# A float32 block on one core: the activation buffers moved to another byte phase relative to the weights

## What is computed

```python
# first block
h = rmsnorm(x, g);   proj = h @ w_in                    # 1024 x 6144
x = x + (gates * (conv, pool and short-conv branches)) @ w_o
x = x + cross_attention(rmsnorm(x), rmsnorm(mem))       # w_xq, w_xkv, w_xo
x = x + moe(rmsnorm(x))      # 16 experts, top 2 of one group: silu(t @ gate) * (t @ up) @ down
x = rmsnorm(x, norm_f_g)
# second block
x = x + rmsnorm((axial attention and gated scan over h @ w_in_2) @ w_out_2)
x = x + rmsnorm(cross_attention_2(...))
x = x + rmsnorm(conv_ffn(...))   # 1024 -> 2 x 2816 -> 3-tap conv -> silu(gate) * val -> 1024
```

## Time and profile before

| | |
|---|---|
| runs, us | 1012.38, 1010.11, 1011.84 |
| median, us | 1011.84 |
| profiled execution: own time, us | 1008.61 |
| its span in the trace, us | 1006.8 |
| TensorE matmul busy | 985.6 us, 98% |
| TensorE weight loads busy | 897.2 us, 89% |
| VectorE busy | 744.3 us, 74% |
| ScalarE busy | 512.7 us, 51% |
| moved by DMA | 178.40 MB, mean 177 GB/s |

### The profile page before, as it was taken

The page is one execution under the profiler, slowest core; times in us unless marked ns, Lnnn a source line. Parts: engine busy times, 40 slices in busy tenths (PEclk is TensorE's granted clock), DMA queues, the critical chain, the costliest instruction groups (busy, mean ns, idle before and its releaser), DMA issues.

```text
span 1006.8 us, 16645 instructions
## 1 busy us (share of the span) xinstructions
PE 985.6 (98%) x6544; PEld 897.2 (89%) x6546; DVE 744.3 (74%) x1118; ACT 512.7 (51%) x746; POOL 53.2 (5%) x55
## 2 busy tenths in 40 slices
PE   7999999999999999999999999999999999999997
PEld 6999998989999888888789899887999989999996
DVE  5699878559756786787859778865476279787876
ACT  3545533414444666676744545445455466454544
POOL 0002001000102100000003000000110120000000
PEclk9999999999999999999999999999999999999999
DMA  7954644455530677887853434111543246555541
GB/s 281 346 173 174 208 131 146 149 176 214 173 123 1 252 263 267 305 281 283 315 208 126 150 118 155 61 64 63 188 165 130 84 153 208 192 179 192 183 167 42
DMA packets 49602, 178.40 MB, mean 177 GB/s; under 512 B 5632, under 2 KB 5888, under 8 KB 49280
## 3 DMA queue, kind: packets, MB, share of 16 engines
q1 hardware_dynamic: 47952, 172.51, 49.4%
q10 hardware_dynamic: 1584, 4.99, 1.4%
HBM read 176.43 MB, written 1.05 MB: 176 GB/s over the span
## 4 chain that ended last, share of the span: by engine, by line
PE 88%; DVE 7%; ACT 2%; DMA 1%; issue 1%; SPq 0%; DVEq 0%; ACTq 0%
PE psum L704 87%; DVE wl L2144 2%; DVE xl L2182 1%; DMA raw<-stream_in 1%; DVE work L2144 1%; PE psum L935 1%; ACT wh L1646 1%; DVE xh L2177 0%; PE psum L1228 0%; DVE xT L2144 0%; DVE rstd L2172 0%; DVE memn L2144 0%; DVE xT L2671 0%; DVE yl L2144 0%; DVE work L3016 0%
## 5 line engine op out<-in xcount | busy, mean ns | idle before, releaser
L1646 ACT CAST wh<-raw 128x1024 fp32r<-128x1024 f32 x288 | 299.0, 1050 | 300.9 <-PE psum L704 258.1
L2144 DVE TENSOR_TENSOR wl<-raw,wh 128x1024 fp32r<-128x1024 f32 x288 | 345.4, 1232 | 74.2 <-ACT wh L1646 71.4
L704 PE MATMUL psum<-xh,wh 128*128 128x256 f32 x968 | 274.5, 284 | 3.2 <-DVE xl L2182 2.1
L704 PE MATMUL psum<-xl,wh 128*128 128x256 f32 x968 | 271.4, 280 | 0.0
L704 PE MATMUL psum<-xh,wl 128*128 128x256 f32 x968 | 271.3, 280 | 0.0
L704 PEld LDWEIGHTS psum<-xh,wh 128*128 128x128 f32 x968 | 182.3, 188 | 7.3 <-DVE xl L2182 2.9
L704 PEld LDWEIGHTS psum<-xl,wh 128*128 128x128 f32 x968 | 182.3, 188 | 0.5
L704 PEld LDWEIGHTS psum<-xh,wl 128*128 128x128 f32 x968 | 182.4, 188 | 0.0
L704 PE MATMUL psum<-wh,slots 128*128 128x512 f32 x320 | 103.3, 396 | 0.0
L704 PE MATMUL psum<-memn,raw 128*128 128x256 f32 x320 | 73.3, 382 | 0.0
L704 PEld LDWEIGHTS psum<-wh,slots 128*128 128x128 f32 x320 | 60.2, 188 | 14.0
(11 more groups left out here) (273 smaller groups left out, 1494.6 us busy)
## 6 DMA issues: line engine op xcount, KB each, us to landing
raw<-stream_in SPq DMA_DIRECT2D x325, 512.0 KB, 4.5
memn<-mem_t_in ACTq DMA_DIRECT2D x2, 1024.0 KB, 9.3
out_rows<-work SPq DMA_DIRECT2D x4, 256.0 KB, 2.2
const<-const_in ACTq DMA_DIRECT2D x1, 581.0 KB, 3.7
xT<-x_t_in SPq DMA_DIRECT2D x2, 256.0 KB, 4.6
xT<-x_t_in ACTq DMA_DIRECT2D x2, 256.0 KB, 5.4
raw<-stream_in SPq DMA_DIRECT2D x2, 256.0 KB, 5.4
mask<-mask_in ACTq DMA_DIRECT2D x1, 512.0 KB, 14.3
```

The source lines that it names most:

```text
L704: return nc.tensor.matmul(out, w, x, start=start, stop=stop, **kw)
L1646: nc.scalar.copy(wh[:, SLOT[c], :], raw[:, c % RAW, :]).then_inc(hi_ready, 1)
L2144: return v.tensor_tensor(out, a, b, op)
```

## The change

`area` moves, and inside it the x, y and hidden operands move. No instruction is added, removed or put in another place: on each of the five engines the list of instructions is the same in both kernels, row by row. Only the addresses in them differ. `area` grows from 84224 to 84480 bytes, `to_line` from 32 to 416.

```diff
         raw = sb("raw", [P, RAW, HW])
+        WEIGHTS_AT = -(-nc.sbuf_base // 32) * 32
         wh = sb("wh", [P, SPLIT, HW], F32R)
...
         PAIR = DK * T
-        X_AT = WORK + 8
-        HID_AT = WORK + 32 + 5 * T
-        Y_AT = WORK + 2 * PAIR + 36
-        sb("to_line", [P, 8 + -(-(-nc.sbuf_base // 32) * 32 + 32) % 128 // 4])
+        LINE = 512
+        X_AT = WORK + LINE // 4 - 8
+        HID_AT = WORK + LINE // 4 + 5 * T
+        Y_AT = X_AT + 2 * PAIR + 4
+        free_at = -(-nc.sbuf_base // 32) * 32 + 32
+        sb("to_line", [P, 8 + (WEIGHTS_AT - free_at) % LINE // 4])
         area_at = nc.sbuf_base
-        assert area_at % 128 == 0, area_at
-        sb("area", [P, Y_AT + 2 * PAIR + 28])
+        assert area_at % LINE == WEIGHTS_AT % LINE, area_at
+        sb("area", [P, Y_AT + 2 * PAIR + 4])
```

## The result

The changed kernel is faster, by half of what was forecast: median 1006.88 us over ten runs, against 1012.82 us for ten runs of the kernel before beside them, a ratio of 0.9945 (95% interval 0.9932 to 0.9958). A second set, on the chip of a later experiment, gave 0.9959 (0.9942 to 0.9977). The forecast was 1000 us against 1011.84, a ratio of 0.988.

The account below looks back on a forecast made before the run. TensorE's start-to-start matmul distance bounds the kernel. Gains of 13.6, 2.4, 2.4, 0.4, 3.0, 1.3 and 0.8 make 24 us; half, 12, off 1008.61, with 3.2 back, gives 1000 us against 1011.84; range 984 to 1018.

Parts of the forecast that it names:

- What bounds the kernel: Whole kernel: TensorE, busy 98% of the span and never short of work for long; start-to-start matmul distance counts.
- That is the sign that the distance in phase matters: TensorE's read streams: rate patterns differ by operand distance; only y (+272) reached 113.3 ns, only `hid` (+256) 226.7.
- the bound ... is 24 us in all; I take half: All matmul kinds: at best rates, 113.3 and 226.7 ns, 24 us gained; half, 12 us, was forecast.
- x and the 512-column kinds going opposite ways: Sign of being wrong: 1 ns on x is 2.9 us, on all the 512-column kinds 1.0 us.
- `slots` below 230 ns: Sign of being right: in the changed profile the 512-column `slots` matmuls, at 233.3 ns, fall below 230.
- the 680 matmuls: Sign of being right: x matmuls in the window 24 to 102 us grow from 667 to 680 or more.
- That small distances are the good ones: New distances -32 (x), -16 (y), 0 (512 columns), not in the trace, were expected to bring a gain.
- the good rate [not] in every stretch: y products at one distance: 113.3 ns in one stretch, 117 and 118.7 in others; a reason for taking half.
- One term: `act` matmuls of the feed-forward steps: 264 at 231.7 ns, gaining 5.0 ns each, 1.3 us.
- The cover: Feed-forward step: TensorE must gain over 3.5 us before VectorE bounds it; VectorE and ScalarE address moves cost nothing.
- Nothing depends on phase: Rival for all stretches: the start alone decides the pattern; 1011.8 us, give or take 2; chance 0.17.
- Equal phases are the bad place: Rival for every product: moving away from half of 512 bytes slows it, 10 us, so 1022; chance 0.28.

Follow-up runs that it names:

- e7: Changed kernel with x, y and `back` moved to distance +112 from the weights; 994.79 us, ratio 0.9840 to the kernel before.
- the probes: Three runs of TensorE alone, without the computation: matmul stretches with operands at varied distances, widths and starts; rates per matmul, no kernel time.
- e5: Changed kernel with x and y moved to distance +32 from the weights; 1003.19 us, ratio 0.9921 to the kernel before.
- e3: Changed kernel with `slots`, `act`, `hid` and x at distance +256, y at +272; 1013.05 us, ratio 1.0016 to the kernel before.
- e4: Changed kernel with x and y moved to distance -64 from the weights; 1000.49 us, ratio 0.9898 to the kernel before.
- e1: Changed kernel with x and y back at +160 and +272, only 512-column operands moved; 1008.25 us, ratio 0.9978 to the kernel before.

## Why the prediction was right and wrong

- **What bounds the kernel: right.** TensorE's distance from start to start, with all else the same. The waits by name stayed, and at e7 some 4 ns less on x and y made the kernel 11 to 12 us faster than the changed one.
- **"That is the sign that the distance in phase matters": right**, and shown: the probes' rates go by the distance, two stretches of `back` over `slots` tell it from the phase, and the kernels at eight placements have the probes' rates. Some stretches had a pattern that the probes didn't show at their distance: x at 120.0 in the earlier trace rows, x at 117.8 in e5, and y at 113.3 at +272 (and one stretch of e3), where the probes had 116.7 and 118.7.
- **"the bound ... is 24 us in all; I take half": the step that failed, by its x and y terms.** The half was spread over all kinds alike. The 512-column kinds gave more than half of their bound, 2.7 + 1.0 + 0.2 of 5.1 us, and x stationary 0.9 of the 2.4 for 256 columns with weights moving. x moving, which held 13.6 of the 24 and so 6.8 of the 12, gave -0.8, and y -0.6. With x and y at nought the measured rates give 4.8 us against the measured 5.6 and 4.1. The prediction named this way of being wrong itself, x and the 512-column kinds going opposite ways; of its signs only `slots` below 230 ns came, while the 680 matmuls were 662 and the step stayed at 16.9 us.
- **That small distances are the good ones: wrong for 256 columns.** It was the author's guess, since the new distances are in no row of before. At equal phase 256 columns run at 120.0, the slowest rate seen; the fast patterns, at 113.3, are at +112, +64 and +192; and the map repeats after 256 bytes, not 512. What came true for 512 columns (226.7 at 0) was expected of 256 columns too, without a row for them. The one row that stood near, `back,slots` at +32 with 118 ns, was weighed too lightly.
- **"the good rate [not] in every stretch": right as far as it goes.** Two patterns at one distance are real (113.3 and 117.8 ns, at +192 in the probes and at -64 in e4). But at -32 and -16 both profiles of the changed kernel show only one, 118.3 and 117.1, and none of its long stretches had 113.3.
- **One term doesn't follow from its rows.** A step of 16.90 us less 96 x 118.7 ns leaves 5.5 us for 24 `act` matmuls, so 229 ns, and not the 231.7 of the prediction. The trace's mean is 232.1, since a step is nearer 16.96 us from start to start. So the term of 1.3 us had the right size, but not from the rows it names.
- **The cover: right.** VectorE and ScalarE took the same time at new addresses, and even at e7's rate the feed-forward steps kept TensorE busy throughout (60.00 of 60.00 us from 840 to 900 us).
- **The rivals.** "Nothing depends on phase" fell with e1, e3 and the probes. "Equal phases are the bad place" is true for 256 columns at exactly 0 or 256 (e3: x at 119.9), false for 512 columns. The "rate below 113.3 that the plain float32 rows hint at" came in no run: plain float32 takes (9.66 - 0.38) / 43 = 215.8 ns for 256 columns, but the lowest settled rates of float32r are 113.3 ns for 256 columns and 226.7 for 512.

## What to carry to other kernels

When TensorE is busy all the time, take the distance from start to start by kind of matmul, stretch by stretch; if one kind differs by some ns at one granted clock, as x did here with 117.3 to 120.0 ns at 1.00, the addresses may be the cause, and a stretch of TensorE alone over a few dozen placements maps that in one run. Here such a map was worth three times the guessed placement: 1.6% against 0.5%. A rate seen at one placement and one width said nothing of another here (at distance 0, 226.7 ns was the best of 512 columns and 120.0 the slowest of 256), and one execution's rates must be seen from several starts, since one placement can have two (113.3 and 117.8 ns at +192).

## What was not expected of the hardware

- float32r matmuls of 256 columns took 113.3 to 120.0 ns at a granted clock of 1.00 and those of 512 columns 226.7 to 240.0, by the distance of the two operands' start bytes modulo 256 and by the width of both. The best of each width, 113.3 and 226.7, are as 1 to 2, so no fixed price of a matmul shows in them. With 512 columns no setting tried reached the 215.8 ns that plain float32 needs for 256.
- A stretch falls into a steady pattern within some ten matmuls and mostly keeps it, up to 670 matmuls long (x at 117.3 ns in the trace of before); at many distances there are two such patterns, and x at +160 and y at +272 showed three (117.3, 118.7 and 120.0; 113.3, 116.7 and 118.7).
- Why it is so stays open. The runs show which distance has which rate, and that a smaller weight load brings no rate below 113.3 and 226.7; they don't show what makes the patterns, nor what a float32r stream does without a weight load beside it.
